# Seven block products in place of eight for the gated linear unit and the feature-major projections

## What is computed

```
    y = jax.nn.gelu(y).astype(u.dtype)
    a, g = jnp.split(y @ w_glu, 2, axis=-1)
    return a * jax.nn.sigmoid(g)
...
        x = x + mix
        x = x + sqrelu_mlp(rmsnorm(x, norm_ffn[i]), mlp_w1[i], mlp_w2[i])
        gate = jax.nn.sigmoid(rmsnorm(x, norm_ple[i]) @ ple_gate_w[i])
        x = x + (p[i] @ ple_w[i]) * gate
    return rmsnorm(x, norm_final)
...
def causal_depthwise_conv(x, w, b):
```

## Time and profile before

| | us |
|---|---|
| median of 3 runs | 3496.84 |
| lowest and highest | 3491.82, 3498.09 |
| the profiled execution | 3494.16 |
| its span in the trace | 3492.1 |
| gated linear unit, block 1 | 339.18 to 515.77 |
| FM tiles 2 to 19, block 1 | 1304.38 to 1500.52 |
| TM, block 1 | 1500.35 to 1656.93 |
| gated linear unit, block 2, starts | 1658.33 |

### The profile page before, as it was taken

How to read it: one execution, slowest core, us unless ns; L and a number is a source line. 1 busy time by engine, 2 the same in 40 slices (tenths; PEclk the granted TensorE clock), 3 DMA queues, 4 the chain that set the end, 5 groups by cost and what they waited for, 6 DMA issues and landing times. The chain is left out here.

```text
span 3492.1 us, 43659 instructions
## 1 busy us (share of the span) xinstructions
PE 3297.7 (94%) x16369; PEld 2687.9 (77%) x16369; DVE 1843.6 (53%) x2234; ACT 1124.5 (32%) x1701; POOL 1442.1 (41%) x1008
## 2 busy tenths in 40 slices
PE   5877999999999999999999999999999999697799
PEld 5656878888888778888887888888778888376687
DVE  8785135555555766970126545454766971455411
ACT  4222133333333541112124333333542111566400
POOL 6710225565666412232325656666412241243522
PEclk9899999999999999999999999999999999898899
DMA  3344211111111213233311111111213231416543
GB/s 124 98 110 125 74 48 49 49 54 48 54 48 54 90 44 127 97 114 119 123 48 49 49 54 48 54 49 53 96 38 121 97 121 58 170 63 211 169 138 116
DMA packets 155667, 301.12 MB, mean 86 GB/s; under 512 B 16512, under 2 KB 91776, under 8 KB 153872
## 3 DMA queue, kind: packets, MB, share of 16 engines
q1 hardware_dynamic: 139376, 257.23, 23.4%
q10 hardware_dynamic: 16160, 42.08, 3.1%
HBM read 226.33 MB, written 72.94 MB: 86 GB/s over the span
## 5 line engine op out<-in xcount | busy, mean ns | idle before, releaser
L1739 PE MATMUL ps_job<-AHL,WH 128*128 128x512 f32 x4480 | 1382.2, 390 | 28.4 <-POOL WL L1298 26.8
L1298 POOL TENSOR_TENSOR WL<-WR,WH 128x1024 fp32r<-128x1024 f32 x216 | 522.8, 2421 | 1204.0 <-ACT WH L996 1202.5
L1739 PEld LDWEIGHTS ps_job<-AHL,WH 128*128 128x128 f32 x4480 | 841.8, 188 | 206.3 <-issue 19.0
L1739 PE MATMUL ps_job<-AHL,WL 128*128 128x512 f32 x2240 | 872.7, 390 | 0.0
L996 ACT CAST WH<-WR 128x1024 fp32r<-128x1024 f32 x216 | 227.0, 1051 | 1006.7 <-PE ps_job L1739 822.8
L1739 PEld LDWEIGHTS ps_job<-AHL,WL 128*128 128x128 f32 x2240 | 421.1, 188 | 88.2
L1494 DVE SCALAR_TENSOR_TENSOR ps_job<-ps_job,RB 128x1024 f32<-128x1024 f32 (+1 forms) x80 | 79.9, 1017 | 409.6 <-PE ps_job L1739 396.2
L1318 POOL TENSOR_TENSOR OPS_L<-VS,OPS_H 128x1024 fp32r<-128x1024 f32 (+2 forms) x96 | 193.7, 2030 | 55.9 <-ACT OPS_H L1122 51.3
L1411 DVE TENSOR_TENSOR VS<-ps_job,VS 128x1024 f32<-128x1024 f32 x16 | 19.6, 1225 | 362.2 <-PE ps_job L1739 362.2
L1671 DVE SCALAR_TENSOR_TENSOR CV<-CU,d_cw,CV 128x1024 f32<-128x1024 f32 x120 | 200.8, 1720 | 0.0
L1836 PE MATMUL ps_job<-OPS_H,WH 128*128 128x512 f32 x512 | 199.5, 390 | 0.7 <-POOL WL L1298 0.7
(11 more groups left out here) (428 smaller groups left out, 5676.7 us busy)
## 6 DMA issues: line engine op xcount, KB each, us to landing
WR<-in_wall SPq DMA_DIRECT2D x244, 512.0 KB, 3.5
fm_scratch<-VS ACTq DMA_DIRECT2D x32, 512.0 KB, 2.6
tm_scratch<-VS ACTq DMA_DIRECT2D x24, 512.0 KB, 2.7
s_U<-in_x_group SPq DMA_DIRECT2D x8, 1024.0 KB, 14.2
s_mt<-z_scratch SPq DMA_DIRECT2D x64, 128.0 KB, 4.5
prod_scratch<-s_Win SPq DMA_DIRECT2D x16, 512.0 KB, 2.6
X<-in_x_feat SPq DMA_DIRECT2D x2, 4096.0 KB, 15.0
m_oz<-tm_scratch SPq DMA_DIRECT2D x8, 1024.0 KB, 8.0
```

The source lines that it names most:

```text
L1298: pool.tensor_tensor(dst, raw, src.bitcast(F32), ALU.subtract).then_inc(raw_free, 1)
L1739: last = pe.matmul(out, l, r, start=(k == 0 and i == 0), stop=(k == k_tiles - 1 and i == 2))
```

## The change

From the third pair on, the pairs of the gated linear unit (6 in each block) and of FM (8 in each block) are computed with seven products of 12 matmuls. Pairs 1 and 2 of either stay as they were. For this

- `win_pair` on TensorE does the products in the order 1, 5, 7, 6, 2, 3, 4 and waits for the low parts of the weights and for readers of PSUM in between;
- `pair_weights` on GpSimd forms four sums of weight blocks and the low parts: eight operations for a pair, of which the last frees both raw buffers at once;
- ScalarE casts the sums (`sums_high`, `last_sum_high`), and copies PSUM halves (`keep_first`, `keep_second`, `keep_fifth`);
- VectorE adds halves (`third_sum`, `corner`, `first_tile`, `second_tile`);
- the right operands T1 to T4 are sums of activation blocks, made once for each stage in YR by VectorE (and for FM four scaled copies on ScalarE), cast by ScalarE (`t_high`) and given low parts by VectorE and GpSimd (`t_low`);
- buffers are shared out anew: MX is single, R1 lies in SG[1], X is stored in three parts, the second half of AH/AL is scratch in the gated linear unit (with the second pair's token halves in the other order), rows 6 and 7 of X and part of VS in FM, and the first gate weights of TM go to G0H/G0L;
- the taps over CU leave the conv tiles: three in silu tiles and in tiles 16 to 27, four from 28 on. The first of the four taps of `convolve` takes its bias as a broadcast operand.

```diff
-TAPS_AT = {j: 3 for j in range(4, 8)} | {j: 2 for j in range(8, 16)} | {j: 3 for j in range(16, N_COPY)}
+TAPS_AT = {j: 3 for j in (*range(4, 8), *range(16, 28))} | {j: 4 for j in range(28, N_COPY)}
...
+                def pair_weights(n, w, b):
...
+                    pool.wait_ge(raw_loaded[0], 16 * w2 + 16)
+                    pool.wait_ge(raw_loaded[1], 16 * w2 + 16)
+                    pool.wait_ge(q6_done, n)
+                    pool.tensor_tensor(raw[:, 0], c[:, 0:HB], c[:, HB:], ALU.add).then_inc(wsum_done, 1)
+                    pool.wait_ge(wsum_done, 4 * n + 1)
+                    pool.tensor_tensor(c[:, 0:HB], a[:, 0:HB], c[:, 0:HB], ALU.subtract).then_inc(wsum_done, 1)
+                    pool.tensor_tensor(raw[:, 1], raw[:, 0], a[:, 0:HB], ALU.subtract).then_inc(wsum_done, 1)
+                    pool.wait_ge(hi_done, w + 1)
+                    pool.tensor_tensor(WL[0][:], a[:], WH[0][:].bitcast(F32), ALU.subtract).then_inc(wl0_done, 1)
...
+                    pool.tensor_tensor(a[:, HB:], a[:, HB:], raw[:, 1], ALU.subtract).then_inc(wsum_done, 1)
...
+                    pool.tensor_tensor(sl[:, 0:2], raw[:, 0:2], sh[:, 0:2].bitcast(F32), ALU.subtract).then_inc(wsl_done, 1)
+                    pool.wait_ge(hi_done, w + 2)
+                    pool.tensor_tensor(WL[1][:], c[:], WH[1][:].bitcast(F32), ALU.subtract).then_inc(wl1_done, 1)
+                    pool.wait_ge(q3_done, n)
+                    pool.wait_ge(wsh_done, 2 * n + 2)
+                    pool.tensor_tensor(sl[:, 2], a[:, HB:], sh[:, 2].bitcast(F32), ALU.subtract).then_inc(raw_free, 2)
...
+                    if not last:
+                        sums_high(n + 1, GLU)
+                    act.wait_ge(q2_done, n + 1)
+                    whi(w0 + m + 1, 0)
+                    keep_fifth(n, GLU, (2 * m + 1) % 4)
...
+                for k in range(KD // 2):
+                    act.activation(YR[:, k], X[:, k], ACT.Copy, scale=gains[:, 3, k:k + 1]).then_inc(x_raw, 1)
                 act.preload_act_table_set("natural_log_exp_and_others")
                 last_norms()
+                act.wait_ge(t_raw, 8 * tb + 8)
+                t_high(2 * tb + 1, range(KD))
...
+                    pe.wait_ge(wl0_done, n + 1)
+                    free(0)
+                    one(1, u, stop=False).then_inc(q1_done, 1)
+                    pe.wait_ge(wsl_done, n + 1)
+                    free(1)
+                    if first:
+                        pe.wait_ge(t_hi, KD * t_set + KD // 2)
+                        pe.wait_ge(t_lo, KD // 2 * (t_set + 1))
+                    one(5, v)
+                    pe.wait_ge(wl1_done, n + 1)
+                    one(7, c)
...
+                    pe.wait_ge(c1_kept, n + 1)
+                    one(6, u, start=False, stop=False).then_inc(q6_done, 1)
+                    one(2, a).then_inc(q2_done, 1)
+                    pe.wait_ge(u2_kept, n + 1)
+                    pe.wait_ge(raw_free, w + 4)
+                    one(3, u, start=False).then_inc(q3_done, 1)
+                    pe.wait_ge(u3_done, n + 1)
+                    one(4, c).then_inc(job_done, 2)
```

More of the change, by code:

```diff
@@ new lines, in _ @@
+                wf = w0 + TILE_FM // 2
+                n = N_WIN * tb + GLU_WIN
+                for j in range(2):
+                    act.wait_ge(job_done, job0 + (JOB_FM + j + 1))
+                    whi(wf + 1, j)
+                    take(j)
+                store_rows(0)
+                act.wait_ge(job_done, job0 + (JOB_FM + 3))
+                whi(wf + 2, 0)
+                store_rows(1)
+                act.wait_ge(st_x[0], 16 * tb + 16)
+                sums_high(n, FM)
+                store_rows(2)
@@ L1259, in _ @@
+                finish_tile(N_FM - 2)
+                take(N_FM - 1)
+                for j in range(TM_AT, N_COPY):
                     for g in range(3):
@@ L1479, in _ @@
+                for k in range(KD - 3):
                     lo_part(0, k)
+                add_up(KD - 3, halves(RB[:]))
+                lo_part(0, KD - 3)
                 for k in range(KD - 2, KD):
```

399 lines of the change are left out of this document (310 added, 89 removed).

## The result

| | before | changed |
|---|---|---|
| median, us | 3497.47 (4 runs) | 3601.59 (4 runs) |
| lowest and highest | 3491.82, 3498.66 | 3598.14, 3604.41 |
| span of the profiled execution | 3492.1 | 3602.7 |
| granted clock over the span | 0.978 | 0.964 |

The ratio is 1.0296, with an interval of 1.0283 to 1.0309. The forecast was 3600 us.

What follows compares the result with a forecast made beforehand. TensorE bounds the kernel before; afterwards a 21.2 us ring without it. Per block -1.1 + 17.1 + 1.5 + 5.5 + 27.9 + 1.9 = 52.8 us; two give 105.6, on 3494.2: 3600 us, range 3500 to 3645.

Steps and rivals of the forecast that it cites:

- a ring of GpSimd, loads and ScalarE: Block pairs of both stages: this loop without TensorE takes 21.2 us a pair, against 19.07 of matmuls.
- rival 1: Block pairs: TensorE stays the bound, pairs take 19.07 us, 3457 us in all, faster; chance 0.05.
- Meetings of two-input operations: Block pairs: a VectorE operation with both inputs in SBUF lengthens each GpSimd operation it meets by 1.0 us.
- The unit: Gated linear unit, six block pairs: 129.7 us against 130.8, so -1.1 us a block.
- The start of FM: Ahead of FM tile 2: T operands and their casts delay its weights, +17.1 us a block.
- The third pair's wait: FM, behind tiles 2 and 3: GpSimd's ten operations each meet one of VectorE's, +5.5 us a block.
- The clock: FM, first matmuls after TensorE's idle time ahead of tile 2: slower at a lower granted clock, +1.5 us a block.
- Edges: Into the token-major stage: two gate tiles come late, +1.9 us a block; from the unit to the MLP 0.
- A sign that came and didn't decide: Block pairs: prediction wrong if something put beside the ring, such as VectorE's third sum, is late on TensorE; no size.
- the eight pairs: FM block pairs: 202.3 us against 174.4, so +27.9 us a block.
- Rival 2: Block pairs: no meetings that count, only the ring of 21.2 us, 3507 us in all; chance 0.11.
- Rival 3: Conv pairs: the clock falls while TensorE idles 8 of 27.2 us, +87 us, 3687 us; chance 0.04.

Runs made afterwards that it cites:

- e3: Changed kernel, but the four taps of each conv tile accumulate in the tile's PSUM slot and ScalarE's silu reads PSUM: 3565.46 us, ratio 1.0199.
- e10: Changed kernel, but in the gated linear unit VectorE writes the product of value and gate back into PSUM: 3588.59 us, ratio 1.0254.
- e2: Changed kernel, but ScalarE casts the next pair's first weight tile before the sums of the weights, in both stages: 3549.38 us, ratio 1.0147.
- e9: Changed kernel with start reordered, tile cast first, conv taps and gate product in PSUM, long-convolution taps late, four plain FM pairs, early plain weights: 3457.79 us.
- e1: Changed kernel, but at FM's start the T operands come behind the norm, tiles 0 and 1, and the weight casts of tiles 2 and 3: 3597.63 us.
- e4: Changed kernel, but all 62 taps of the long convolution lie in the token-major stage, five a tile: 3585.39 us, ratio 1.0246.

## Why the prediction was right, and where it was only right in sum

- **TensorE isn't the bound of a block pair; a ring of GpSimd, loads and ScalarE is.** Right. The bare period of 21.2 us was measured at 21.4 (e3) and 21.2 (e10), taking ScalarE's casts out of it took 2.3 us (e2, 2.1 in the sum), and with casts and meetings out the unit's pairs take 19.2 us in e9, against TensorE's 19.07. One reason that the prediction gave against rival 1, that a load has never been under 3.6 us, was a misreading: the two loads of the earlier trace rows were that slow, but over the whole trace a load of this kind takes 3.3 to 13.8 us, 3.5 in the median. The rival fell all the same.
- **Meetings of two-input operations, 1.0 us for each of GpSimd's.** Right: 26.7 against 27.2 at conv tiles, six operations lengthened by 0.8 to 1.0 us as counted, gone in e3; one in the unit, gone in e10. The pair ahead of the silu work took 22.0 us and the two silu ones 23.3 and 25.7, against 23.2, 24.2 and 24.2. The rule of the Trainium skill that the prediction cites ("SBUF — State Buffer", who interferes with whom) is what e3 and e10 test: same operations, one input moved to PSUM, and GpSimd is back at its own time. The trace agrees.
- **The unit, -1.1 forecast, +5.9 measured.** The mis-sized term. The first pair was to have its weights made ahead, 20.0 us; its WL ended at 387.9, just as TensorE came (388.0), because the four T low parts stand ahead of it on GpSimd, and the period was 22.3. The last took 23.1, not 20.9, and one pair 23.6:

```profile
440.09 1.26 POOL L1469 TENSOR_TENSOR AHL<-WR,AHL 128x512 fp32r<-128x512 f32 x1
448.06 1.29 POOL L1453 TENSOR_TENSOR B_L<-WR 128x512 f32<-128x512 f32 x1 [6.70 <-PE ps_job L2096]
...
415.17:431.79 16.62, 16.62 (x72) 13.45 (x72) 2.09 (x3) 3.16 (x5) 8.71 (x6) 1.00 0.19 64
437.84:456.04 18.20, 18.20 (x72) 14.58 (x72) 2.09 (x3) 3.79 (x5) 9.31 (x6) 0.91 0.17 59
...
506.37:522.90 16.53, 16.53 (x66) 13.49 (x67) 10.19 (x8) 6.05 (x8) 7.55 (x3) 0.90 0.19 63
```

  In the 23.6 us pair the first sum came 6.70 us behind the last low part and was released by TensorE: a way from the low sums through products 5, 7 and 6, which the prediction didn't have. Its matmuls went at a lower clock, 72 in 18.20 us at 0.91 against 16.62 at 1.00 in the pair ahead. The unit is the same code in e1, e3 and e4; there all five full periods stand at 1.00, none of the first sums waits for TensorE, and they take 21.9 to 22.7 us. The last pair's matmuls went at 0.90.
- **The start of FM, +17.1 forecast, 18.2 measured.** Right. The twelve operations of 512 columns lie 0.68 us apart and not 0.62, which makes 0.7 of the difference; GpSimd's WL of tile 2 took 4.2 us and not 3.4, the rest. What the prediction said of it, that tile 2's weights stand behind the T operands, is true and would have misled whoever mends only that: e1.
- **The third pair's wait, 5.5 forecast, 1.1 measured.** The step that failed is the count of ten meetings. Eight of GpSimd's ten operations met one, and the first WL ended 24.7 us behind tile 2's start and not 27.4; tiles 2 and 3 took 23.6 us and not 21.8, which the forecast had counted as a term of its own and not against this wait.
- **The clock, +1.5.** Right where the wait stands: 23.6 and 22.05 us for the same 96 matmuls behind 19.8 and 1.6 us of waiting.
- **Edges.** +2.2 against +1.9 at the token-major stage; +1.9 where I had put 0, from the unit's end to FM, is not at the unit's edge (27.0 us from there to the MLP's first plain matmuls before, 26.9 after). It lies in the last 305 us, where the granted clock was 0.99 and then 0.98 against 1.00 before. Why it was lower isn't known.
- **A sign that came and didn't decide.** The prediction called itself wrong if VectorE's third sum was late on TensorE. It was, by 3.6 us in each conv pair, and the period of GpSimd's ring hid it; in e2, with a shorter ring, it came out.

So the sum was nearer than its terms, which is luck: 7 us too little in the unit and 2 between it and FM stand against 4 too much at the third pair and 2 in the eight pairs. And of the 110.6 us between the two spans 3.3 are in a stage that the change doesn't touch; the medians are 104.1 us apart.

Rival 2, no meetings, was refuted by e3 and e10; rival 1, TensorE as the bound, is what e9 makes of the unit. Rival 3, a falling clock, happened in part and was mostly covered by the ring.
